# Experts ordered on the chip: full ones and light ones of 64 rows in turn, gate and up loaded in 4 KB rows

## The reference

```python
def moe_swiglu(x, w_router, w_gate, w_up, w_down):
    logits = (x @ w_router).astype(jnp.float32)
    top_val, top_idx = lax.top_k(logits, TOP_K)          # TOP_K = 2
    wts = jax.nn.softmax(top_val, axis=-1)
    gates = jnp.sum(jax.nn.one_hot(top_idx, N_EXPERTS, dtype=jnp.float32) * wts[..., None], axis=-2)
    out = jnp.zeros_like(x)
    for e in range(N_EXPERTS):                           # N_EXPERTS = 8
        h = jax.nn.silu(x @ w_gate[e]) * (x @ w_up[e])   # w_gate, w_up: 1024 x 3584
        out = out + gates[..., e:e + 1].astype(x.dtype) * (h @ w_down[e])   # w_down: 3584 x 1024
    return out
```

## Time and profile before

| what | value |
|---|---|
| device time, median of 3 runs | 1814.25 us (1811.07 to 1816.32) |
| span of the profiled execution | 1810.5 us |
| TensorE busy | 1727.4 us (95%) |
| VectorE busy | 1408.4 us (78%) |
| ScalarE busy | 1040.0 us (57%) |
| moved by DMA | 531.18 MB, mean 293 GB/s |
| mean granted clock of TensorE | 0.983 |

### The profile page before, as it was taken

One profiled execution on the slowest core, in us unless ns is written; L12 is line 12 of the kernel. 1 busy time (PEld: TensorE's weight loads), 2 busy tenths in 40 slices (PEclk: granted clock), 3 DMA queues, 4 the chain that ended last, 5 costly groups with the idle time before them and its releaser, 6 DMA issues.

```text
span 1810.5 us, 22521 instructions
## 1 busy us (share of the span) xinstructions
PE 1727.4 (95%) x9346; PEld 1470.9 (81%) x9346; DVE 1408.4 (78%) x1241; ACT 1040.0 (57%) x850; POOL 54.0 (3%) x44
## 2 busy tenths in 40 slices
PE   3999999998889999998999999999999999999997
PEld 3988788878679997996888888888888888888885
DVE  7796667665975554777988879989888898898897
ACT  2344444453243332434777767777777777777773
POOL 0000002000000000002000000000000000000110
PEclk9999999999989999998999999999999999999998
DMA  9687255614737574563999999999999999999993
GB/s 363 237 335 294 91 178 181 257 59 154 203 141 278 187 260 159 209 225 137 387 404 377 392 374 374 384 374 390 384 376 387 371 384 385 373 393 376 376 400 129
DMA packets 220460, 531.18 MB, mean 293 GB/s; under 512 B 10288, under 2 KB 16704, under 8 KB 220096
## 3 DMA queue, kind: packets, MB, share of 16 engines
q1 hardware_dynamic: 213312, 514.53, 77.3%
q10 hardware_dynamic: 5712, 10.41, 1.6%
q0 software_dynamic: 1328, 4.73, 0.8%
HBM read 521.94 MB, written 16.09 MB: 297 GB/s over the span
## 4 chain that ended last, share of the span: by engine, by line
PE 75%; DVE 3%; ACT 1%; issue 1%; POOL 0%; DVEq 0%; POOLq 0%; ACTq 0%
PE psum L822 23%; PE psum L824 23%; PE psum L823 23%; PE psum L1259 1%; PE psum L1149 1%; DVE units L1783 1%; DVE R L2183 0%; PE psum L1102 0%; PE psum L1218 0%; PE psum L1228 0%; PE psum L935 0%; PE psum L1187 0%; POOL root_out L1732 0%; PE psum L1120 0%; PE psum L1110 0%
## 5 line engine op out<-in xcount | busy, mean ns | idle before, releaser
L1783 DVE TENSOR_TENSOR units<-ring,units 128x2048 fp32r<-128x2048 f32 x451 | 1013.2, 2278 | 196.3 <-ACT units L1386 133.6
L1657 ACT CAST units<-ring 128x2048 fp32r<-128x2048 f32 x332 | 633.6, 1916 | 214.2 <-PE psum L824 214.2
L822 PE MATMUL psum<-units,xr 128*128 128x512 f32 x1120 | 441.9, 395 | 1.8 <-DVE xr L1783 1.4
L824 PE MATMUL psum<-units,xr 128*128 128x512 f32 x1120 | 436.7, 390 | 0.0
L823 PE MATMUL psum<-units,xr 128*128 128x512 f32 x1120 | 436.0, 389 | 0.0
L1386 ACT CAST units<-ring 128x2048 fp32r<-128x2048 f32 (+1 forms) x119 | 218.6, 1881 | 213.6 <-PE psum L824 184.7
L822 PE MATMUL psum<-units,H 128*128 128x512 f32 x696 | 274.8, 395 | 4.4 <-DVE H L1783 4.4
L823 PE MATMUL psum<-units,H 128*128 128x512 f32 x696 | 272.5, 392 | 0.0
L824 PE MATMUL psum<-units,H 128*128 128x512 f32 x696 | 272.5, 392 | 0.0
L822 PE MATMUL psum<-xr,units 128*128 128x256 f32 x864 | 248.6, 288 | 4.5 <-DVE xr L1783 3.2
L822 PEld LDWEIGHTS psum<-units,xr 128*128 128x128 f32 x1120 | 210.3, 188 | 47.1 <-issue 5.3
(11 more groups left out here) (278 smaller groups left out, 993.3 us busy)
## 6 DMA issues: line engine op xcount, KB each, us to landing
ring<-in_moe_w_gate SPq DMA_DIRECT2D x112, 1024.0 KB, 8.7
ring<-in_moe_w_up SPq DMA_DIRECT2D x112, 1024.0 KB, 8.8
ring<-in_moe_w_down SPq DMA_DIRECT2D x112, 1024.0 KB, 7.8
ring<-in_mod_w SPq DMA_DIRECT2D x12, 2048.0 KB, 9.6
ring<-in_ret_w_in SPq DMA_DIRECT2D x11, 2048.0 KB, 9.6
ring<-in_fox_w_in SPq DMA_DIRECT2D x8, 2048.0 KB, 8.4
ring<-in_sc_w_in SPq DMA_DIRECT2D x6, 2048.0 KB, 8.2
ring<-in_ffn_w_gate SPq DMA_DIRECT2D x5, 2048.0 KB, 7.9
```

The source lines that it names most:

```text
L822: mm(dst, left[0], right[0], start=first, stop=False)
L824: return mm(dst, left[1], right[0], start=False, stop=last)
L1657: nc.scalar.copy(*expert_unit_parts(q, j, half, 0)).then_inc(unit_high, 1)
L1783: return v.tensor_tensor(dst, src, high.bitcast(F32), ALU.subtract)
```

## The change

Three of the eight experts become "light". VectorE sorts the experts by their token count (`experts_in_order`). Expert 0 stays first. The others are placed so that the three with the fewest tokens come at positions 2, 4 and 6, with 64 rows of room instead of 128; all others keep 128. SP reads the expert's number of each position from `order`. If an expert has more tokens than its room, everything runs a second time.

In a light expert the stationary side holds the 64 rows' high part and low part side by side (128 columns). So there are two matmuls to a product (with the weights' high and low part) instead of three, and 64 x 128 results more are made in the lower half of the bank (low x low is included). The two halves have to be added: ScalarE copies gate and up to `e_s` and `e_ht`, and TensorE multiplies each block of 128 columns with `fold` (two identities of 64), which adds and turns in one. That takes the place of the four transposes: 8 float32 products of 64 columns a chunk. Silu, product, high and low part follow on 256 columns instead of 512. The sums of a light expert are folded by two products of 512 columns in the next expert.

Gate and up are loaded as one chunk of 512 columns and then three slabs of 1024 columns (4 KB rows), 2 blocks of input rows a half. Each half is used for two banks, and gate (4 halves) and up (4 halves) of a slab follow each other. `high` and `low_unit` go over halves instead of pairs of them; what is done between the halves is put down by the functions `gate_out`, `up_out` and `turn_after`.

The core of the diff:

```diff
-GATHER_AFTER = 7
-ROWS_BEFORE = 8
+GATHER_AFTER = 18
+ROWS_BEFORE = 16
...
+LIGHT = (2, 4, 6)
+LROWS = P // 2
+FIRST_LIGHT = NE - len(LIGHT)
+ROOMS = [LROWS if p in LIGHT else P for p in range(NE)]
...
+def slab_of(c):
+    return (c + 1) // 2
+def gate_end(c):
+    return 8 * slab_of(c) if c else 2
+def up_end(c):
+    return 8 * slab_of(c) + 4
+def gate_out(c):
+    return gate_end(c) + 3
+def up_out(c):
+    return up_end(c) + 3
+def turn_after(c, light):
+    second = 1 if c and c % 2 == 0 else 0
+    return up_end(c) + (2 if light else 4) + second
+def half_source(h):
+    if h < 4:
+        return "gate" if h < 2 else "up", 4 * (h % 2), 4, 0, COLS
+    if h < 4 * PAIRS:
+        slab, r = divmod(h - 4, 8)
+        return "gate" if r < 4 else "up", 2 * (r % 4), 2, COLS * (1 + 2 * slab), 2 * COLS
+    return "down", 2 * (h - 4 * PAIRS), 2, 0, D
...
+                if number == 1:
+                    of = e - NE
+                elif e == 0:
+                    of = 0
+                else:
+                    sp.wait_ge(order_ready, 1)
+                    of = sp.value_load(order[0:1, e:e + 1], min_val=0, max_val=NE - 1)
...
+                    sp.wait_ge(unit_ready, e * EH + 2 * PRE + h + 1 - HALVES)
+                    kind, k0, n, at, width = half_source(h)
+                    if kind == "down":
+                        src = t["moe_w_down_2"][0].rearrange("e (r p) n -> e p r n", p=P)[bass.ds(of, 1), :, k0:k0 + n, :]
+                        dst = as_rows(ring[:, expert_slot(h), :], n)
+                    else:
+                        w = t["moe_w_gate_2"] if kind == "gate" else t["moe_w_up_2"]
+                        src = w[0].rearrange("e (k p) n -> e p k n", p=P)[bass.ds(of, 1), :, k0:k0 + n, at:at + width]
+                        dst = as_cols(ring[:, expert_slot(h), :], n)
+                    sp.dma_start(dst, src.rearrange("o p k n -> (o p) k n")).then_inc(half_filled[expert_slot(h)], 16)
...
+            def light_product(dst, left, right, first, last):
+                mm(dst, left, right[0], start=first, stop=False)
+                return mm(dst, left, right[1], start=False, stop=last)
...
+            def gate_or_up(e, q, kind, slab, light, first=False, after=None):
+                chunks = [0] if slab == 0 else [2 * slab - 1, 2 * slab]
+                up = kind == "up"
+                pe.wait_ge(up_emptied if up else gate_emptied, e * PAIRS + chunks[0] + 2)
+                banks = [psum[:, 4 + 2 * up + c % 2, :] for c in chunks]
+                begin = (up_end if up else gate_end)(chunks[0]) - 2 * len(chunks)
+                for h in range(begin, begin + 2 * len(chunks)):
+                    if first and h == 1:
+                        pe.wait_ge(gather_emptied, 1)
+                    _, k0, n, _, _ = half_source(h)
+                    w = expert_unit(e, q, h, lambda a: as_cols(a, n))
+                    for k in range(n):
+                        kk = k0 + k
+                        for c, b in enumerate(banks):
+                            right = [a[:, k, c * COLS:(c + 1) * COLS] for a in w]
+                            if light:
+                                last = light_product(b, e_xl[q][:, kk, :], right, kk == 0, kk == KB - 1)
+                            else:
+                                last = product(b, [a[:, kk, :] for a in e_x[q]], right, kk == 0, kk == KB - 1)
+                    last.then_inc(expert_used, 1)
+                    if after is not None:
+                        after(h)
...
+                def fold_hidden(c):
+                    pe.wait_ge(gate_emptied, e * PAIRS + c + 3)
+                    pe.wait_ge(up_emptied, e * PAIRS + c + 3)
+                    b = turn_bank(c)
+                    for i, src in enumerate((e_s, e_ht)):
+                        for j in range(4):
+                            at = (4 * i + j) * LROWS
+                            last = mm(b[:, at:at + LROWS], src[:, c % 2, j * P:(j + 1) * P], fold, start=True, stop=True)
+                    last.then_inc(turn_filled, 1)
+                def fold_rows():
+                    pe.wait_ge(down_emptied, e + 1)
+                    for c in range(2):
+                        last = mm(psum[0:LROWS, c, :], fold, y_row[:, c * 512:(c + 1) * 512], start=True, stop=True)
+                    last.then_inc(fold_filled, 1)
...
+            def high(e, q, h):
+                base = h % EH
+                act.wait_ge(half_filled[expert_slot(base)],
+                            (e + h // EH) * (16 * EH // HALVES) + 16 * (base // HALVES + 1))
+                act.wait_ge(expert_used, e * EH + h - UNITS + 1)
+                dst, src = expert_unit_parts(q, h, 0)
+                nc.scalar.copy(dst, src).then_inc(unit_high, 1)
...
+                def light_silu(c):
+                    act.wait_ge(turn_filled, turns(e, number) + c + 1)
+                    if c >= 2:
+                        act.wait_ge(light_hidden, PAIRS * lights_before(e) + c - 1)
+                    nc.scalar.activation(l_s[:, c % 2, :], turn_at(c, q, number)[:, 0:4 * LROWS], ACT.Silu).then_inc(light_gated, 1)
+                def light_high(c):
+                    act.wait_ge(light_hidden, PAIRS * lights_before(e) + c + 1)
+                    nc.scalar.copy(e_h[0][:, 4 * c:4 * c + 4, 0:LROWS], l_h[:, c % 2, :].rearrange("p (j n) -> p j n", j=4)
+                                   ).then_inc(turn_high, 1)
...
+                        if h == gate_out(c):
+                            gated(c)
+                        if light and h == up_out(c):
+                            upped(c)
+                        if light and h == t_c + 4:
+                            light_silu(c)
+                        if light and h == t_c + 5:
+                            light_high(c)
...
+            def experts_in_order():
+                q = [sort_t[:, i] for i in range(8)]
+                step(v.scalar_tensor_tensor(q[KEY], counts[:, :], float(NE), desc, ALU.mult, ALU.add))
+                step(v.tensor_scalar(q[KEY][:, 0:1], q[KEY][:, 0:1], float(NE * 2 * T + NE), None, ALU.add))
+                step(v.tensor_tensor(sort_c, across(q[KEY]), down_rows(q[KEY]), ALU.is_gt))
+                step(v.tensor_reduce(q[RANK], sort_c, AX.X, ALU.add))
+                step(v.tensor_scalar(q[BEHIND], q[RANK], float(FIRST_LIGHT), float(1 - NE), ALU.is_ge, ALU.mult))
+                step(v.scalar_tensor_tensor(q[POS], q[RANK], 2.0, q[BEHIND], ALU.mult, ALU.add))
+                step(v.tensor_scalar(q[POS], q[POS], -1.0, 0.0, ALU.add, ALU.max))
+                step(v.tensor_scalar(room[:, :], q[RANK], float(FIRST_LIGHT), float(LROWS - P), ALU.is_ge, ALU.mult))
+                step(v.tensor_scalar(room[:, :], room[:, :], float(P), None, ALU.add))
+                step(v.tensor_tensor(sort_c, across(q[POS]), down_rows(iota), ALU.is_equal))
+                step(v.tensor_tensor(sort_c, sort_c, across(iota), ALU.mult))
+                step(v.tensor_reduce(q[KEY], sort_c, AX.X, ALU.add))
+                v.tensor_copy(order[:, :], q[KEY][0:1, :]).then_inc(order_ready, 1)
+                step(v.scalar_tensor_tensor(q[IN], q[RANK], float(P + LROWS), room[:, :], ALU.mult, ALU.add))
+                step(v.scalar_tensor_tensor(q[IN], room[:, :], float(SHORT), q[IN], ALU.mult, ALU.add))
+                step(v.tensor_scalar(q[IN], q[IN], float(-SHORT * P - P - LROWS), 0.0, ALU.add, ALU.max))
+                step(v.tensor_scalar(q[IN], q[IN], -1.0, None, ALU.add))
+                step(v.scalar_tensor_tensor(q[EXTRA], desc, -float(P), room[:, :], ALU.mult, ALU.subtract))
+                step(v.scalar_tensor_tensor(q[EXTRA], q[EXTRA], float(MAIN + NE * P - 1), q[IN], ALU.add, ALU.subtract))
+                step(v.tensor_scalar(q[LAST], q[POS], float(NE - 1), None, ALU.is_equal))
+                step(v.tensor_tensor(q[SPILL], counts[:, :], room[:, :], ALU.subtract))
...
+                def multiplied(c):
+                    dve.wait_ge(gate_emptied, e * PAIRS + c + 3)
+                    dve.wait_ge(expert_used, e * EH + up_end(c))
+                    v.tensor_tensor(e_ht[:, c % 2, :], e_s[:, c % 2, :], psum[:, 6 + c % 2, :], ALU.mult).then_inc(up_emptied, 1)
...
+                def light_multiplied(c):
+                    dve.wait_ge(light_gated, PAIRS * lights_before(e) + c + 1)
+                    v.tensor_tensor(l_h[:, c % 2, :], l_s[:, c % 2, :], turn_at(c, q, number)[:, 4 * LROWS:8 * LROWS], ALU.mult
+                                    ).then_inc(light_hidden, 1)
+                def light_low(c):
+                    dve.wait_ge(turn_high, e * PAIRS + c + 1)
+                    low(e_h[0][:, 4 * c:4 * c + 4, LROWS:P], l_h[:, c % 2, :].rearrange("p (j n) -> p j n", j=4),
+                        e_h[0][:, 4 * c:4 * c + 4, 0:LROWS]).then_inc(turn_emptied, 1)
...
+            experts_in_order()
+            for_last(slot_of)
+            for_last(gate_of)
```

(46 more changed lines are left out.)

328 lines of the change are left out of this document (178 added, 150 removed).

## The result

The changed kernel takes 1781.26 us (median of 4 runs, 1780.15 to 1784.13) against 1815.02 us of the kernel before in the same series: a ratio of 0.9822, 95% interval 0.9808 to 0.9836. The forecast was 1784 us.

What follows compares the result with a forecast made beforehand. TensorE was taken to bound the kernel, with DMA and VectorE close behind. Span 1810.5 - 35.1 (three pairs) + 5.0 (sorting) = 1780.4 us, plus 3.75 to the median: 1784 us; range 1768 to 1803 us.

Steps and rivals of the forecast that it cites:

- Three limits close together: Per expert before the change: TensorE 118.7 us, DMA about 116 us, VectorE 103.8 us; TensorE relief alone saves 3 us.
- The light expert: Forecast 105 us: TensorE's work 89.6, ScalarE's 95, VectorE's 100.9, DMA limit 100.1, plus 4 us for the in-order chain.
- TensorE idle for some 15 us: Sign expected in a light expert: TensorE idle that long, released by VectorE's low halves, with VectorE busy over 95%.
- The price of the queues' order: Light expert's chunks pass TensorE, ScalarE and VectorE on in-order queues: bounded at 0 to 1.2 us a chunk, 4 us taken.
- The DMA: Full plus light expert: 89.7 MB, 4 KB rows at 408 GB/s and 2 KB rows at 389, 220.8 us a pair.
- The credit of a full expert: Halves lying ready in the ring and converted places let the DMA run ahead: up to 11 us for the light expert.
- The full expert behind a light one: Four float32 records folding the light expert's sums add 2.0 us, making 120.7 us.
- The start: Sorting adds 24 small VectorE instructions before the low part of half 4, 5.0 us, all on the path.
- The DMA at its old rate: Rival: 4 KB rows give nothing in the experts, a pair takes 230.5 us, total 1799 us; chance 15%.
- Full overlap: Rival: the light expert takes only VectorE's 100.9 us, total 1772 us, or 1769 with a cheaper sums fold; chance 10%.
- The serial chain: Rival: TensorE's fold waits for ScalarE's copies in each chunk, light expert 126 us, total 1847 us; chance 7%.
- The clock: Rival: TensorE waiting for DMA in every half drops to half clock, light expert 179 us, total 2006 us; chance 4%.

Runs made afterwards that it cites:

- the three-pass run: Changed kernel with all experts computed in three passes on 128 columns, new load order (4 KB rows) and sorting kept: 1821.39 us, ratio to before 1.0048.
- with less to load: Changed kernel, each half of down in light experts loaded to one half only (512 KB instead of 1 MB): 1771.93 us, one run.
- The run with the turn one half later: Changed kernel with late sums; in expert 7 the selection and last chunk turned behind half 34 instead of 33: 1772.18 us, ratio to before 0.9769.
- the one with both: Changed kernel with late sums, expert 7's last turn one half later, and returned rows behind halves 18 and 27: 1770.46 us, ratio to before 0.9763.
- the run with 2 KB rows: Changed kernel, light experts kept, gate and up loaded in 2 KB rows as before the change: 1801.29 us, ratio to before 0.9939.
- the doubled fold: Changed kernel with each of the 56 folding products of a light expert done twice: 1795.28 us, one run.
- late sums: Changed kernel, start of sums, overflow test and its load moved from before half 4 of expert 0 to behind halves 6, 8, 9: 1774.19 us, ratio 0.9794.

## Why the prediction was right

The mechanism held: three limits close together, the pair of experts bounded by the DMA's total, and a light expert that lives on the lead of the full one. That the sum came within 3 us is in part luck: the light experts were 9.6 us better than forecast, the start, the end and the full experts 7.5 us worse.

*Three limits close together.* Right. TensorE alone faster with the old rows gave 0.6%, the rows alone nothing. The sign that was read for it, a share of 1.03, is weaker than it looked, since the three-pass run has 1.01 with time to spare; the rate decides.

*The light expert.* Forecast 105 us, measured 101.3 to 102.1. TensorE's work was put at 89.6 us and is 89 us by starts: 336 x 0.227, seven folds of 1.7 us, and 0.9 us of transposes.

```profile
1102.89 1.89 PE L1363 MATMUL psum<-const,R 128*128 128x64 f32 x16
1104.60 0.48 PE L1304 MATMUL psum<-units,xr 128*128 128x512 f32 x1
```

The sign "TensorE idle for some 15 us" has to be read the same way: 101.8 - 89 is 13 us of waiting, of which the profile lists 5 as idle.

The term that was too high is VectorE's, put at 100.9. By starts a low half costs 2.20 us, not 94.8 / 42 = 2.26, and an instruction of 256 columns 0.33 us, about the 0.35 forecast:

```profile
1140.91 8.89 DVE L1972 TENSOR_TENSOR units<-ring,units 128x2048 fp32r<-128x2048 f32 x4
1149.72 0.42 DVE L2707 TENSOR_TENSOR R<-R,psum 128x256 f32<-128x256 f32 x1
1150.05 2.29 DVE L1972 TENSOR_TENSOR units<-ring,units 128x2048 fp32r<-128x2048 f32 x1
```

That makes 42 x 2.20 + 14 x 0.33 + 1.1, about 98 us. The price of the queues' order, 4 us, I had to take between 0 and 8; with less to load the light expert is at 99.1 to 99.5, so it is about 1 us. The other 2.5 us up to 101.8 are the DMA's.

*The DMA.* 408 GB/s was the forecast from the program's start, 406 and 400 are measured in a light and a full expert, 403 over the pair of 222.5 us, against a forecast of 220.8 us of DMA. The Trainium skill's 425 GB/s for a core that streams alone ("HBM Reference", Specifications) was not reached over any 10 us of the changed kernel; the most were 422 GB/s over 10 us (from 867.5 us) and 409 over 100 us (from 1640 us). The credit of a full expert exists and is as large as worked out: the light expert behind a full one is 102 us, one behind a light one 110 to 113, what its 44.6 MB take at 400 GB/s.

*The full expert behind a light one.* Forecast 120.7, measured 121.2. The fold of the sums is 1.9 us of it:

```profile
L1370 PE MATMUL psum<-R,const 128*64 128x512 f32 x4 | 1.9, 605 | 0.0
```

The rest is two waits of 0.7 and 0.2 us at its start. The new order costs nothing in a full expert otherwise (118.5 us), as said.

*The start.* The wait was forecast at 5.0 us more and is 5.0 us more. Missing was the clock: behind the wait TensorE runs at half clock for a while, 1.5 us more (6.5 in all). Taking 3.0 us of VectorE's block away gave 4.3 us: 3.0 of wait and 1.3 of clock.

*The end.* This is the term that the prediction did not have: +7.2 us in expert 7, of which the fold of the sums, 2.0 us, was priced. The waits at its start, 0.7 us, were not, and neither were the other 4.5 us, the wait of 3.0 us and the half clock behind it, 1.5. The additions of the returned rows and the last chunk's turn were moved by the change, from behind halves 15, 23 and 31 to 24, 34 and 33, and the emptying of chunk 5's bank from behind half 31 to 36; I walked through the new order for a plain full expert only. The run with the turn one half later, and the one with both, show the whole of it: 125.1 and 124.6 us.

Together: light experts 3 x 3.2 = 9.6 us better than forecast, start and end 6.0 us worse, the three full ones behind light ones 0.5 us worse each: -32.2 instead of -30.1 us.

*The rivals.* The DMA at its old rate is what the run with 2 KB rows is: 1801 us, forecast 1799. Full overlap (100.9 us) came near by its number only: VectorE's work is 98 us, and the light expert stays nearly 4 us above it. The serial chain is excluded by the doubled fold. The clock did not fall in a light expert (1.00 in the windows), though TensorE has some ten short waits in each, up to 1.3 us; so what the Trainium skill ("TensorE: Matmul & The Clock Gate", HAM oscillation) tells of a kernel that waits for DMA in every step is not seen there. Half clock was seen behind single longer waits, and not behind all of them. No second pass over the experts was needed.

## What to carry to other kernels

Where two limits lie within a few per cent, a change to one of them must be priced against the other, and each half of such a change measured alone looks like almost nothing. Work that differs from stage to stage is best interleaved, so that the buffers of a rich stage carry the poor one; what a stage can borrow is what lies ready in the ring, here 8 to 11 us. Where durations overlap, price and read an engine by the distance between starts: short waits do not show as idle time. And a change of a hand-written order has to be walked through in its special stages too, the first and the last: these took 11 of the 51 us back, and moves of a few instructions gave 9 of them again.

## What the runs showed of the hardware

Behind a wait of TensorE of 5.4 us at the start its clock was at half in all seven runs that have this wait, and not behind the waits of 2.5 us in the four runs with late sums. In expert 7, half clock followed a wait of 3.0 us in the changed kernel, with less to load, with late sums and with the fold twice, but not in the three-pass run; and it followed 1.9 us in both runs that have that wait. So the length of the wait alone does not tell. The half clock lasted some 3.4 us, at a cost of about 1.5 us. In the run with less to load and in the one with 2 KB rows it lasted longer in expert 0 (0.50 in the windows from 860 to 866 us and from 858 to 864 us), which took 126.9 us instead of 125.8.

With 4 KB rows the DMA moved 400 to 409 GB/s at a share of 1.03, with 2 KB rows 387 to 395 at 1.04, under the same work of the engines. In the three-pass run it moved 383 GB/s at 1.01 without holding anything up.
